# Expert blocks: a second low-part split on GpSimd, and the bias products one slab later

## The reference, cut to what matters

```python
logits = xf @ router_w + router_b
top_logit, top_idx = lax.top_k(logits, 4)          # 4 of 32 experts for each of 1024 tokens
gate = softmax(top_logit)
# for each expert e, for its tokens x:
gu = x @ w_gate_up[e] + b_gate_up[e]               # 1024 -> 2048
g, u = minimum(gu[:, :1024], 7), clip(gu[:, 1024:], -7, 7)
act = (u + 1) * (g * sigmoid(1.702 * g))
y = act @ w_down[e] + b_down[e]                    # 1024 -> 1024
out[tokens] += y * gate
```

## Time and profile before

| | us |
|---|---|
| median of 3 runs | 2639.85 (2631.32 to 2643.12) |
| the profiled execution | 2638.29 |
| its span, first to last instruction | 2636.7 |
| mean granted TensorE clock, share of full speed | 0.946 |
| TensorE busy | 2372.2 (90%) |
| VectorE busy | 1606.5 (61%) |
| ScalarE busy | 1310.4 (50%) |
| GpSimd busy | 907.4 (34%) |

### The profile page before, as it was taken

How to read it: one execution, slowest core, us unless ns; L and a number is a source line. 1 busy time by engine, 2 the same in 40 slices (tenths; PEclk the granted TensorE clock), 3 DMA queues, 4 the chain that set the end, 5 groups by cost and what they waited for, 6 DMA issues and landing times.

```text
span 2636.7 us, 39181 instructions
## 1 busy us (share of the span) xinstructions
PE 2372.2 (90%) x13878; PEld 1822.8 (69%) x13879; DVE 1606.5 (61%) x1526; ACT 1310.4 (50%) x1453; POOL 907.4 (34%) x654
## 2 busy tenths in 40 slices
PE   6989999999998889029999999999999999999995
PEld 5857768777786768017777777777777777777774
DVE  4034353544423432727878887878888878777785
ACT  4145454554534421025655665556566556555554
POOL 1210101011011100762545454545465535434453
PEclk9988989999898989559999999999999999999998
DMA  3000201111114432348888998889899888887884
GB/s 128 25 25 21 65 22 41 47 30 58 36 57 156 138 136 104 94 150 307 323 290 304 344 326 290 303 297 367 280 367 347 280 290 319 291 281 273 298 303 149
DMA packets 277825, 524.72 MB, mean 199 GB/s; under 512 B 39041, under 2 KB 87228, under 8 KB 277596
## 3 DMA queue, kind: packets, MB, share of 16 engines
q1 hardware_dynamic: 244028, 476.21, 50.9%
q0 software_dynamic: 22208, 43.38, 6.9%
q10 hardware_dynamic: 11520, 4.20, 0.6%
HBM read 480.34 MB, written 47.56 MB: 200 GB/s over the span
## 4 chain that ended last, share of the span: by engine, by line
PE 41%; POOL 6%; issue 5%; DMA 3%; ACT 1%; DVE 1%; POOLq 0%; DVEq 0%; ACTq 0%
PE ex_gu L1790 23%; PE ex_yp L1834 8%; PE ex_rest L1812 4%; DMA ex_nxt<-slots 3%; PE ex_rest L1851 2%; POOL ex_idx L1576 2%; PE ex_gu L1783 1%; POOL slots L1563 1%; ACT ex_whi L1491 1%; POOL ex_nxt L1571 1%; POOL ex_sel L1618 1%; PE ex_tr L1751 1%; DVE ex_hlo L1681 1%; PE ex_yp L1827 0%; ACT ex_hhi L1510 0%
## 5 line engine op out<-in xcount | busy, mean ns | idle before, releaser
L1648 DVE TENSOR_TENSOR ex_wlo<-ex_raw,ex_whi 128x2048 fp32r<-128x2048 f32 x355 | 804.6, 2291 | 179.1 <-ACT ex_whi L1491 177.9
L1491 ACT ACTIVATE ex_whi<-ex_raw 128x2048 fp32r<-128x2048 f32 x387 | 736.0, 1920 | 311.9 <-PE ex_gu L1790 224.4
L1790 PE MATMUL ex_gu<-ex_whi,ex_xhi 128*128 128x512 f32 x1024 | 333.9, 407 | 5.4 <-DVE ex_wlo L1648 5.4
L1790 PE MATMUL ex_gu<-ex_wlo,ex_xhi 128*128 128x512 f32 x1024 | 321.0, 395 | 0.0
L1790 PE MATMUL ex_gu<-ex_whi,ex_xlo 128*128 128x512 f32 x1024 | 319.6, 393 | 0.0
L603 POOL TENSOR_TENSOR at_wlo<-at_raw,at_whi 128x1024 fp32r<-128x1024 f32 x32 | 79.6, 2487 | 583.8 <-ACT at_whi L448 583.8
L1629 POOL TENSOR_TENSOR ex_wlo<-ex_raw,ex_whi 128x2048 fp32r<-128x2048 f32 x32 | 148.0, 4625 | 251.9 <-ACT ex_whi L1491 251.9
L1790 PEld LDWEIGHTS ex_gu<-ex_whi,ex_xhi 128*128 128x128 f32 x1024 | 192.2, 189 | 58.0 <-DVE ex_wlo L1648 7.4
L1790 PEld LDWEIGHTS ex_gu<-ex_whi,ex_xlo 128*128 128x128 f32 x1024 | 193.9, 189 | 43.9
L1790 PEld LDWEIGHTS ex_gu<-ex_wlo,ex_xhi 128*128 128x128 f32 x1024 | 193.6, 189 | 42.9
L56 PE MATMUL at_job<-xnT_hi,at_whi 128*128 128x512 f32 x448 | 196.1, 438 | 0.0
(11 more groups left out here) (256 smaller groups left out, 4198.7 us busy)
## 6 DMA issues: line engine op xcount, KB each, us to landing
ex_raw<-in_w_gate_up_dram SPq DMA_DIRECT2D x512, 512.0 KB, 7.0
ex_raw<-in_w_down_dram SPq DMA_DIRECT2D x256, 512.0 KB
at_raw<-in_w_in_dram SPq DMA_DIRECT2D x28, 512.0 KB
gT<-at_gst SPq DMA_DIRECT2D x32, 256.0 KB, 2.4
mg_g<-gT SPq DMA_DIRECT2D x32, 256.0 KB, 3.1
n_x<-in_x_dram SPq DMA_DIRECT2D x8, 512.0 KB, 8.1
mg_ytok<-y_s SPq DMA_DIRECT2D x16, 256.0 KB, 4.2
raw_o<-in_w_out_dram SPq DMA_DIRECT2D x8, 512.0 KB, 6.6
```

Of the source, the lines that this page charges most:

```text
L1491: nc.scalar.activation(w_hi[:, i % RING, :], raw[:, i % SLABS, :], ACT.Copy).then_inc(hi_d, 1)
L1648: nc.vector.tensor_tensor(w_lo[:, slot, :], raw[:, i % SLABS, :], w_hi[:, slot, :].bitcast(F32), ALU.subtract).then_inc(lo_d, 1)
L1790: mm = nc.tensor.matmul(gu[:, half, h, :], x[:, k, :], w[:, kk, h, :], start=k == 0 and n == 0, stop=k == KD - 1 and n == 2)
```

## The change

Three things. `POOLED` becomes a pair: GpSimd makes the low parts of slabs 10 and 11, one right behind the other, and VectorE's split of slab 11 goes. TensorE's wait counts follow. The gate/up bias products move from in front of slabs 2 and 6 to in front of slabs 3 and 7 (and those of the rest rows in the same way). The down bias stays where it is.

```diff
-POOLED = 10
+POOLED = (10, 11)
@@ GpSimd, body
-                hold(pool, hi_d, SLABS * b + POOLED + 1, spare)
                 hold(pool, piece_d, b + 1, spare)
-                slot = POOLED % RING
-                nc.gpsimd.tensor_tensor(w_lo[:, slot, :], raw[:, POOLED, :], w_hi[:, slot, :].bitcast(F32),
-                                        ALU.subtract).then_inc(lo_pool, 1)
+                for i in POOLED:
+                    hold(pool, hi_d, SLABS * b + i + 1, spare)
+                    nc.gpsimd.tensor_tensor(w_lo[:, i % RING, :], raw[:, i, :], w_hi[:, i % RING, :].bitcast(F32),
+                                            ALU.subtract).then_inc(lo_pool, 1)
                 next_rows(b + 2)
@@ VectorE, body
                 activate_rest(b)
-                split_lo(b, 11)
                 hidden_lo(b, 1)
@@ TensorE
-                if i == POOLED:
-                    pe.wait_ge(lo_pool, b + 1)
+                if i in POOLED:
+                    pe.wait_ge(lo_pool, 2 * b + i - 9)
                 else:
-                    pe.wait_ge(lo_d, (SLABS - 1) * b + i + (1 if i < POOLED else 0))
+                    pe.wait_ge(lo_d, 10 * b + i + 1)
@@ gate_up
-                if pair_of_k == 2:
-                    if i == 2:
+                if pair_of_k == 3:
+                    if i == 3:
                         pe.wait_ge(sel_d, b + 1)
```

## The result

| | median, us | runs | ratio to before, 95% interval |
|---|---|---|---|
| before | 2641.11 | 2631.32 to 2643.12 | |
| changed | 2683.99 | 2682.07 to 2684.95 | 1.0169 [1.0143, 1.0195] |

The changed kernel is slower by 43 us (1.7%), clear of the scatter of either. Its profiled execution took 2683.5 us (span 2681.9, 45.2 more than the span of before).

The account below looks back on a forecast made before the run. The prediction took TensorE, busy 1381.6 of 1416 us in the expert stage, as the bound. Its terms, 60.6 + 24 - 3.4 - 10 = +71 us on 2638.3, gave 2709 us, range 2674 to 2748.

Parts of the forecast that it names:

- (c): TensorE's transposes L1759 wait for L1674: 2.4 us net in 14 blocks, 1.5 in 18, together +60.6 us.
- (d): TensorE's granted clock falls behind 14 gaps of 3.6 us: +24 us, less 3.4 for today's two falls.
- (e): Gate/up bias products one slab later: waits for the selector fall from 14.6 to 4.4 us, -10 us.
- E: In each block of the expert stage, the end of GpSimd's split of slab 10, from which times are counted.
- short blocks: The 14 of 32 expert blocks without over-full rows, each with a 1.28 us wait before slab 10; +2.4 us each forecast.
- long ones: The 18 of 32 expert blocks with extra rest products and no wait before slab 10; +1.5 us each forecast.
- Rival 1: L1674 is blocked by GpSimd's second split, but TensorE's clock holds: 2685 us; chance 0.17.
- Rival 3: L1674 slips in front of GpSimd's second split or is not held; bias waits stay near 14.6: 2622 us; chance 0.08.
- The bound: In the expert stage, no change leaving TensorE's own work alone gains more than its waits of 17.9 and 14.6 us.

Follow-up runs that it names:

- experiment with the PSUM operand: Changed kernel, but L1670 writes its clamped values back to PSUM, so L1674 reads one PSUM and one SBUF tile; 2648.07 us, ratio 1.0051.
- run with the filled gap: Changed kernel plus ten extra bf16 products in TensorE's order before the transposes L1758, in blocks without over-full rows alone; 2671.35 us, ratio 1.0123.
- best kernel of the experiments: Changed kernel with L1674 on one PSUM input and the index instruction and row gathers moved behind the next selector and additions; 2599.83 us, ratio 0.9853.

## Why the prediction was right, and where it was off

**The mechanism** was right in its main steps; what was off are the sizes of (c) and (d). L1674 was held in 32 of 32 blocks, until 0.28 us after the end of the second split (0.29 forecast). GpSimd's second split came behind L1662, not in front of it. TensorE waited at the transposes behind it, in all blocks, and the experiment with the PSUM operand took this away. Splitting off the bias move showed that it gains.

**The sum** was 71 and the measured difference is 43. By parts, from the waits of TensorE and the run with the filled gap:

| | forecast | measured |
|---|---|---|
| (c) wait for L1674, less that for L1681 | +60.6 | 64.1 + 2.4 - 17.9 = +48.6 |
| (d) clock | +24 - 3.4 = +20.6 | 12.6 + 4.6 - 3.4 = +13.8 |
| (e) bias waits | -10 | 0.6 - 14.6 = -14.0 |
| sum | +71 | +48.4 |

(The 3.4 us of the two falls of before are the forecast's reading of the earlier trace rows, not measured apart. The 4.6 are the waits for the selector, 5.2 less 0.6, that stand in the filled kernel where the falls stood.) Against this sum stands the time from the first of these transposes to the last, 1389.3 us before and 1437.9 after, so 48.6 more (the first row is the kernel before, the second the changed one; the last two numbers ahead of the form are the first and the last start):

```profile
L1759 PE MATMUL ex_gu<-ident,ex_hid x64: 272/273/330, 1211.7 to 2601.0; 128*128 128x128 f32 x64
L1758 PE MATMUL ex_gu<-ident,ex_hid x64: 272/327/476, 1207.6 to 2645.5; 128*128 128x128 f32 x64
```

The spans differ by less, 45.2, mostly because TensorE reached the stage 3 us earlier in the changed kernel's profiled execution (its first gate/up product starts at 1166.0 and not 1169.0), and the medians by 43; this is scatter of the stages before, which the change doesn't touch.

*Part (c)* is the term that was furthest off in us, by 12. It missed that the bias products of slab 6 had stood in front of what releases the split of slab 10. With them behind slab 6, E comes earlier against TensorE's own order: L1750 starts at 1298.06 = E + 1.76, where L1751 started at 1477.02, E + 1.21, before. This shortens every gap by what E gained, 2.93 instead of 3.56 us in short blocks and 1.20 instead of 1.5 in long ones. In the long ones the second split also ended later (E + 5.5) since slab 11's high part did not come earlier with E. Putting the bias back raised the wait for L1674 by 5.7 us, so this is the direction, though not all of the 12 us.

*Part (d)* had the price of a fall right and the number of those that count wrong. From one L1758 to the next the changed kernel and the filled one take the same time within 0.02 us wherever no fall lies between. Two such stretches of the changed kernel, each from a short block's transposes to the next long block's, the first without a fall and the second with one (columns as in the earlier trace rows):

```profile
1394.50:1440.96 46.46, 45.07 (x304) 33.26 (x307) 37.55 (x26) 26.73 (x21) 26.46 (x16) 1.00 0.91 312
...
1484.56:1532.63 48.07, 46.52 (x303) 34.54 (x306) 37.70 (x26) 27.07 (x21) 27.28 (x16) 0.96 0.89 302
```

The fall costs 1.6 us, against 1.7 in the forecast. But 3 of the 14 gaps had none, and four falls lay between two short blocks, where TensorE would otherwise have waited for the selector (the 5.2 us of the filled kernel): the four such stretches together are only 0.9 us longer than there. Two falls in front of long blocks lasted twice as long and cost 2.8 us each. The forecast added the falls and the bias waits, (d) and (e), as if one did not hide the other.

*Part (e)* expected 4.4 us to remain, in 4 waits, and 0.6 did. GpSimd was late as forecast: without the falls there are 4 waits with 5.2 us. In the changed kernel TensorE was later too, by the falls.

**Rival 1** gave the right time from "the clock holds". It did not hold: it fell beside 11 of the 14 long gaps. Its number came out by luck, as (c), (d) and (e) were all lower than forecast.

**Rival 3**, L1674 not held, was priced at 2622. With the PSUM operand this was tested: 2648 and unstable. The selector's wait was taken to stay near 14.6 us; 30.8 stood in its fastest run. The forecast of a later GpSimd had each held instruction wait for one known run of splits; that it can miss this and be held by the next was not foreseen.

**The bound** of 32.5 us on any gain counted the waits alone and not the clock falls behind them. The best kernel of the experiments gained 38 us by its median, of which 32.8 lie between the first and the last of the rest rows' transposes (1356.4 us there, 1389.2 before); the rest came before or behind them.

## What to carry to other kernels

Before work goes from VectorE to GpSimd, list every VectorE instruction with two SBUF inputs that falls into the new instruction's time, and ask who waits for it; a small one on the critical path can cost nearly the whole length of the GpSimd instruction (here 0.42 us became 3.9 to 4.4, beside a split of 4.6), and one operand left in PSUM freed it. Ask the reverse as well: a short GpSimd instruction in front of something urgent (here the selector) can be held for VectorE's whole run of back-to-back two-input instructions, so put the urgent one first. And where an instruction is only late in its engine's order, exchange it with its neighbour before giving work to another engine.

## What the runs showed of the hardware

- GpSimd did not get the port pair at the border between two VectorE splits that were queued back to back. In a run of four (8.88 us) a 128x1 instruction waited 6.85 us, to the run's end. The other way round VectorE did get in between GpSimd's two splits, in the short blocks, where both were ready.
- An indirect DMA that GpSimd issues is held in the same way: 7.41 us behind a run of three splits, where in the kernel before it took 1.1 to 3.0 us. The Trainium skill ("SBUF — State Buffer", section "SBUF: two separate sides") tells of descriptors held up by VectorE's copies that use both ports, and says that `tensor_tensor` did not hold up a DMA. Here a run of VectorE's `tensor_tensor` with two SBUF inputs did, and the measurement decides. Whether it held the writing of the descriptors or GpSimd's reading of the row numbers (`ex_nxt`) is not shown.
- Gaps of TensorE of one length have unlike effects on the clock. In the 6 us around the end of three gaps of 2.93 us the mean granted clock was 0.57, 0.76 and 1.00. A single fall cost TensorE 1.6 us of dense work, and next to nothing where TensorE would have had to wait for another engine anyway.
